# A hybrid diffusion step on one core: low-rank inputs with ScalarE a tile ahead, and two merge branches made inside the recurrent output's stage

## What is computed

```
z = modulate(x, shift1, scale1) @ w_in
z_rw, z_cv, z_q, z_k, z_v, z_gate = split(z)
# recurrent branch, per direction d:
z_rw = z + mu_prev * (z_prev - z) + mu_next * (z_next - z)      # token shift
decay = exp(-0.607 * sigmoid(rw_w0[d] + tanh(zw) @ rw_w2[d]))
a     = sigmoid(rw_a0[d] + za @ rw_a2[d])
k_d   = k * (1 + (a - 1) * rw_k_a)
bonus = sum(r * k * rw_r_k) * v ;  kk = normalize(k * rw_k_k)
y_rw  = (group_norm(scan(...)) + bonus) * (sigmoid(zg) @ rw_g2)
# merge
g_a, g_b, g_c = split(sigmoid(z_gate))
merged = g_a*(y_rw @ w_out_rwkv) + g_b*(y_cv @ w_out_conv) + g_c*(y_at @ w_out_attn)
x = x + gate1 * (merged @ w_o)
x = x + gate2 * peer_ffn(modulate(x, shift2, scale2))
```

## Time and profile before

| what | us |
|---|---|
| median of the runs | 6358.67 |
| lowest and highest of 3 runs | 6358.47, 6360.23 |
| the profiled execution's own time | 6360.67 |
| its span, first to last instruction | 6358.8 |
| PE busy in the span | 5276.5 |
| DVE busy | 3789.7 |

### The profile page before, as it was taken

One profiled execution on the slowest core, in us unless ns is written; L12 is line 12 of the kernel. 1 busy time (PEld: TensorE's weight loads), 2 busy tenths in 40 slices (PEclk: granted clock), 3 DMA queues, 4 the chain that ended last, 5 costly groups with the idle time before them and its releaser, 6 DMA issues. The chain is left out here.

```text
span 6358.8 us, 68926 instructions
## 1 busy us (share of the span) xinstructions
PE 5276.5 (83%) x25836; PEld 2786.5 (44%) x25836; DVE 3789.7 (60%) x8443; ACT 1299.4 (20%) x3116; POOL 1496.5 (24%) x1408
## 2 busy tenths in 40 slices
PE   7998799896987877778789987998968877777777
PEld 3555488453333333333345554884533333333333
DVE  3544566435677777777534445664256777777775
ACT  1022211112222222222111222111022222222221
POOL 0100000002444444444300000000024444444443
PEclk9999899998999899989999998998989999999998
DMA  3112501335999999999831135113359999999998
GB/s 126 67 58 110 215 31 47 147 116 225 420 420 419 406 419 413 417 410 414 356 110 65 58 128 197 40 39 148 115 238 420 420 419 411 418 409 417 410 419 354
DMA packets 325587, 1664.17 MB, mean 262 GB/s; under 512 B 36072, under 2 KB 69096, under 8 KB 159616
## 3 DMA queue, kind: packets, MB, share of 16 engines
q0 software_dynamic: 193504, 1370.70, 52.3%
q1 hardware_dynamic: 131744, 289.00, 12.5%
HBM read 1585.80 MB, written 73.79 MB: 261 GB/s over the span
## 5 line engine op out<-in xcount | busy, mean ns | idle before, releaser
L2008 PE MATMUL psum<-peer_rows,peer_diagonal 128*128 128x512 f32 x5120 | 2512.5, 643 | 703.5 <-ACT peer_diagonal L2052 703.5
L1960 POOL DMA_INDIRECT peer_rows<-in_peer_rows,peer_index x1280 | 1428.8, 1116 | 3361.3 <-PE psum L2008 1737.7
L2151 DVE CUSTOM_DVE_ANT_0 peer_rows<-peer_rows,h_rows 128x1024 f32<-128x1024 f32 x1280 | 1546.7, 1224 | 839.9 <-DMA peer_rows<-in_peer_rows,peer_index 836.8
L2008 PEld LDWEIGHTS psum<-peer_rows,peer_diagonal 128*128 128x128 f32 x5120 | 1020.3, 205 | 2116.2 <-issue 1211.5
L2052 ACT ACTIVATE peer_diagonal<-ident_sb,peer_weight 128x128 f32<-128x128 f32 x1280 | 409.3, 390 | 705.0 <-DVE peer_weight L2123 698.2
L2046 ACT ACTIVATE peer_active<-peer_dots 128x4 f32<-128x4 f32 x320 | 65.7, 205 | 1643.1 <-DVE peer_dots L2151 1643.1
L468 PE MATMUL psum<-in_weights,h_sb 128*128 128x512 f32 (+1 forms) x800 | 309.9, 549 | 0.0
L968 PE MATMUL psum<-h_sb,rw_in_gate_weights 128*128 128x512 f32 (+1 forms) x768 | 232.1, 469 | 84.3 <-ACT y_rw L1003 57.9
L521 DVE SCALAR_TENSOR_TENSOR conv_acc<-conv_in,conv_taps,conv_acc 128x655 f32<-128x655 f32 x240 | 216.4, 901 | 8.5
L468 PEld LDWEIGHTS psum<-in_weights,h_sb 128*128 128x128 f32 x800 | 152.0, 190 | 158.1 <-issue 154.0
L968 PEld LDWEIGHTS psum<-h_sb,rw_in_gate_weights 128*128 128x128 f32 x768 | 133.5, 220 | 187.1 <-issue 94.1
(11 more groups left out here) (345 smaller groups left out, 6167.5 us busy)
## 6 DMA issues: line engine op xcount, KB each, us to landing
rw_out_mod_weights<-in_w_mod SPq DMA_DIRECT2D x16, 2048.0 KB
in_weights<-in_w_in SPq DMA_DIRECT2D x12, 2048.0 KB, 8.5
peer_rows<-in_peer_rows,peer_index POOLq DMA_INDIRECT x1280
modulation_weights<-in_w_mod SPq DMA_DIRECT2D x8, 2048.0 KB
scratch_rw_scratch<-rw_in_direction SPq DMA_DIRECT2D x20, 768.0 KB, 3.6
wkv_own<-scratch_rw_scratch SPq DMA_DIRECT2D x20, 768.0 KB, 6.8
merge_gates<-scratch_gate_scratch SPq DMA_DIRECT2D x16, 960.0 KB
rw_in_gate_weights<-in_w_gate POOLq DMA_DIRECT2D x24, 512.0 KB, 6.0
```

Source lines behind the costliest of these rows:

```text
L1960: nc.gpsimd.indirect_dma_start(rows[spot][:, :], None, t.dram["peer_rows"], bass.IndirectOffsetOnAxis(ap=index[j % 4][:, k:k + 1], axis=0) ...
L2008: last = nc.tensor.matmul(t.bank[2 * (i % 2) + c], diagonal[k % DIAGONALS][:, :], rows[spot][:, D + c * 512:D + (c + 1) * 512], start=(j = ...
L2151: v.tensor_tensor_reduce(rows[spot][:, 0:D], rows[spot][:, 0:D], h[:, :], 1.0, 0.0, ALU.mult, ALU.add, dots[b][:, k:k + 1]).then_inc(s["do ...
```

## The change

It has two parts, and a moved buffer.

1. **Inputs.** The token shift of the low-rank rows moves into the attention stage: DVE does it in six pieces between the units (three instructions a piece, into the new tile `lora_mixed`). In the inputs' stage PE adds the rows `W0` and `A0` itself, by a matmul with one row of ones after each low-rank matmul, so that the two adds of DVE go and ACT reads PSUM. ACT's order becomes: sigmoids, scales, copy of the g2 product, empty(2i), square, root, the low-rank tile of the next token tile, empty(2i+1). DVE makes the bonus's products while ACT squares. PE's first gate comes alone, and products(i) is followed by gate(2i+1) and gate(2i+2).
2. **Output and merge.** The convolution and attention branches of the merge (conv, attn) are made in the output's stage, one block of columns before each chunk of the modulation; DVE gates them into `t.merged`. The modulation's weights get two buffers for four. The merge's stage keeps the recurrent branch alone: 4 matmuls for each i and g, with the weights and gates loaded in two parts.

```diff
@@ attention_stage
+        LORA_UNITS = [(HEADS + 1 + 3 * n, j, g) for n, (j, g) in enumerate((j, g) for j in range(3) for g in range(2))]
+            sp.dma_start(mu_lora[:, :, :], t.dram["mu_lora"][layer, :, :, :]).then_inc(s["mu_loaded"], 16)
+            def shift_lora(j, g):
+                (lo, m), at = GROUPS[g], LORA_PAD[g]
+                out = t.lora_mixed[:, j, lo:lo + m]
+                shifted.step(nc.vector.tensor_scalar(out, t.lora[:, j, at:at + m], mu_lora_own[:, j:j + 1], None, ALU.mult))
+                for k, begin in enumerate((at - 1, at + 1)):
+                    shifted.step(nc.vector.scalar_tensor_tensor(out=out, in0=t.lora[:, j, begin:begin + m], scalar=mu_lora[:, k, j:j + 1], in1=out,
+                                                                op0=ALU.mult, op1=ALU.add))
...
@@ rwkv_inputs_stage
-                if i:
-                    pe.wait_ge(s["vector"], VECTOR.after("a1", i - 1))
-                for d in range(2):
-                    b = d * HD
-                    nc.tensor.matmul(t.bank[d][:, :], lora_tile[b:b + HD, 0, :], w2[b:b + HD, :], start=True, stop=True)
-                for d in range(2):
-                    b = d * HD
-                    nc.tensor.matmul(t.bank[2 + d][:, :], lora_tile[b:b + HD, 1, :], a2[b:b + HD, :], start=True, stop=True)
+                for first, row, j, low_rank in ((2, A0, 1, a2), (0, W0, 0, w2)):
+                    for d in range(2):
+                        b = d * HD
+                        nc.tensor.matmul(t.bank[first + d][:, :], lora_tile[b:b + HD, j, :], low_rank[b:b + HD, :], start=True, stop=False)
+                        nc.tensor.matmul(t.bank[first + d][:, :], t.ones[0:1, :], rows[0:1, row + d, :], start=False, stop=True)
...
             for i in range(TILES):
+                act.wait_ge(s["products"], i + 1)
                 if i:
+                    act.wait_ge(s["vector"], VECTOR.after("key1", i - 1))
+                for d in range(2):
+                    nc.scalar.activation(a[:, d, :], t.bank[2 + d][:, :], ACT.Sigmoid).then_inc(s["scalar"], 1)
...
-                    done.step(v.tensor_tensor(per[d][:, 0, :], t.bank[d][:, :], rows[:, W0 + d, :], ALU.add))
-                    done.step(v.tensor_tensor(a[:, d, :], t.bank[2 + d][:, :], rows[:, A0 + d, :], ALU.add))
@@ rwkv_output_stage
-        mod_weights = [sbuf(f"mod_weights{b}", KD, 512) for b in range(4)]
+        gates, out_weights, product = both("gates", 2, NTOK), both("out_weights", 2, 4, P), sbuf("product", LAT)
+        mod_weights = [sbuf(f"mod_weights{b}", KD, 512) for b in range(2)]
...
+            def load_branch(n):
+                if n >= 2:
+                    sp.wait_ge(s["branch"], 3 * (n - 1))
+                sp.dma_start(out_weights[n % 2][:, :, :, :], t.dram["w_out"][layer, n, :, 1:3, :, :]).then_inc(weights_loaded[n % 2], 16)
+                if n >= 2:
+                    sp.wait_ge(s["gated"], 6 * (n - 1))
+                sp.dma_start(gates[n % 2][:, :, :], t.dram["gate_scratch"][3 * n + 1:3 * n + 3, :, :].rearrange("r p n -> p r n")).then_inc(gates_loaded[n % 2], 16)
...
+            for n in range(KD):
+                load_branch(n)
+                if n == 0:
+                    sp.dma_start(rows[:, :, :], t.dram["rw_rows"][layer, 7:9, :].partition_broadcast(P)).then_inc(s["rows_loaded"], 16)
+                if n < TILES:
+                    load_tile(n)
+                modulation_load(sp, t, s, layer, chunks, mod_weights, mod_bias, n)
...
+            for n in range(KD):
+                branch(n)
+                modulation_product(nc, pe, t, s, chunks, mod_weights, mod_bias, n)
+                if n:
+                    modulation_spread(nc, pe, t, s, chunks, mod_rows, pick, n - 1)
+                if 1 <= n <= TILES:
+                    turn(n - 1)
...
+            for n in range(KD):
+                act.wait_ge(gates_loaded[n % 2], 16 * (n // 2 + 1))
+                nc.scalar.activation(gates[n % 2][:, :, :], gates[n % 2][:, :, :], ACT.Sigmoid).then_inc(s["sigmoid"], 1)
+                if n < TILES:
...
+                modulation_copy(nc, act, t, s, mod_rows, n)
+                if n:
+                    modulation_store(nc, act, t, s, chunks, n - 1)
@@ merge_stage
-        units = [(i, g, r) for i in range(KD) for g in range(2) for r in range(3)]
+        units = [(i, g) for i in range(KD) for g in range(2)]
+        parts = ((0, FIRST), (FIRST, KD))
```

More of the change, by code:

```diff
@@ L1697, in turn, with gate @@
                 dve.wait_ge(s["turned"], i + 1)
-                v.tensor_copy(t.y_rw[:, :, i * P:(i + 1) * P], t.bank[i % 2].rearrange("p (j n) -> p j n", j=4)).then_inc(s["y_copied"], 1)
+                v.tensor_copy(t.y_rw[:, :, i * P:(i + 1) * P], turn_bank.rearrange("p (j n) -> p j n", j=4)).then_inc(s["y_copied"], 1)
+            def gate(n):
+                dve.wait_ge(s["sigmoid"], n + 1)
+                for r, (g, source) in enumerate((g, source) for g, source in ((1, branch_banks), (0, (context_bank[:, 0:P], context_bank[:, P:2 * P])))):
+                    lo, m = GROUPS[g]
+                    out = t.merged[:, n, lo:lo + m]
+                    dve.wait_ge(s["branch"], 3 * n + (1 if g else 3))
+                    v.tensor_tensor(out, gates[n % 2][:, 0, lo:lo + m], source[0][:, 0:m], ALU.mult).then_inc(s["gated"], 1)
+                    if g:
+                        dve.wait_ge(s["branch"], 3 * n + 2)
+                    dve.wait_ge(s["gated"], 6 * n + 3 * r + 1)
+                    v.tensor_tensor(product[:, 0:m], gates[n % 2][:, 1, lo:lo + m], source[1][:, 0:m], ALU.mult).then_inc(s["gated"], 1)
+                    dve.wait_ge(s["gated"], 6 * n + 3 * r + 2)
+                    v.tensor_tensor(out, out, product[:, 0:m], ALU.add).then_inc(s["gated"], 1)
+                dve.wait_ge(s["gated"], 6 * n + 6)
             for i in range(TILES):
+                gate(i)
                 done = Steps(dve, s["vector"], i * len(VECTOR.names))
@@ L1721, in _ @@
                     turn(i - 1)
+            gate(TILES)
             turn(TILES - 1)
+            for n in range(TILES + 1, KD):
+                gate(n)
             dve.wait_ge(s["y_copied"], TILES)
-RWKV_OUTPUT = ("rows_loaded", "loaded0", "loaded1", "turned", "vector", "scalar", "picked", "y_copied", *MOD_SIGNALS)
+RWKV_OUTPUT = ("weights_loaded0", "weights_loaded1", "gates_loaded0", "gates_loaded1", "branch", "gated", "sigmoid", "rows_loaded", "loaded0", "loaded1", "turned", "vector", "scalar", "picked", "y_copied", *MOD_SIGNALS)
 def merge_stage(nc, t, s, before, layer):
-    UNITS = 6
     BANKS = 8
+    FIRST = 2
     with ExitStack() as mem:
@@ L1767, in _ @@
         def _(pe):
-            for n, (i, g, r) in enumerate(units):
+            for n, (i, g) in enumerate(units):
                 lo, m = GROUPS[g]
-                if n % UNITS == 0:
-                    pe.wait_ge(weights_loaded[i % 2], 16 * (i // 2 + 1))
+                if g == 0 and i in (0, FIRST):
+                    pe.wait_ge(weights_loaded[i // FIRST], 16)
                 if n >= BANKS:
@@ L1774, in _ @@
                 for k in range(4):
-                    last = nc.tensor.matmul(t.bank[n % BANKS][:, 0:m], out_weights[i % 2][:, r, k, :], branches[r][:, k, lo:lo + m],
-                                            start=(k == 0), stop=(k == 3))
+                    last = nc.tensor.matmul(t.bank[n % BANKS][:, 0:m], out_weights[:, i, k, :], t.y_rw[:, k, lo:lo + m], start=(k == 0), stop=(k == 3))
                 last.then_inc(s["product"], 1)
             pe.wait_ge(s["gated"], len(units))
-            pe.wait_ge(s["added"], KD * 4)
+            pe.wait_ge(s["added"], len(units))
             pe.wait_ge(s["last_loaded"], 32)
```

206 lines of the change are left out of this document (97 added, 109 removed).

## The result

The changed kernel takes 6390.47 us (median of 5 runs, 6386.47 to 6396.73) beside 6359.51 for the kernel before (5 runs on the same chip): a ratio of 1.0044, 95% interval 1.0033 to 1.0056. It is 31 us slower, where 40 us less had been forecast. Its profiled execution took 6396.73 us, with a span of 6395.0.

A forecast was written before the change was run, and what follows sets the result against it. PE bounds attention, output and merge; in the inputs' stage engines take turns, and PE would set the pace after the change. Saving 2 x (12.0 + 7.7) = 39.4 from 6360.67 gives 6321.3 profiled, median 6319, range 6294 to 6341.

The forecast's parts named there:

- rival 3: Inputs' stage: PE still waits 29.0 us for copies out of bank 7; +9.3 us a layer, median 6377; chance 0.04.
- the 3 us either way: Output and merge stages: the margin given to their net -7.7 us a layer, for moved turns and chunk 0's landing.
- the one-row term: Inputs' stage, low-rank products: nine matmuls of alternating shapes run in series at 0.96 us each, 8.6 us a tile.
- the forecast 148.7: Inputs' stage, PE's first to last gate: 12 x 8.65 + 5 x 8.6 + 1.9 = 148.7 us, against 160.7 before.
- Rival 2: Inputs' stage: clock falls once a tile in the low-rank products, making them 10.7 us; -9.2 a layer, median 6340; chance 0.08.
- Rival 1: Inputs' stage: one-row matmuls overlap, products 6.1 us a tile; -32.2 us a layer in all, median 6294.3; chance 0.26.

The follow-up runs named there:

- the spreads apart: Changed kernel with identity bias matmuls first, plus the output stage's modulation spread moved ahead of the next chunk's product: 6296.99 us, 0.9891 of the kernel before.

## Why the prediction was wrong

**What held.** PE's waits for `y_rw` went, 29.0 to 0 (rival 3 did not come). PE became the stage's bound. Output and merge: the merge fell by 70.4 us (forecast 69.3), the output's stage grew by 63.0 (61.6), net -7.4 against -7.7 in the first layer. Chunk 0's product began 16.1 us after the stage's first transfer (forecast 15.9), since its weights landed about when forecast (16.1 for 15.7); PE's first matmul came after 3.6 us and not 5.1, and PE then waited 1.9 us for these weights. Attention stayed within 0.1 us, and DVE's shift there cost 8.4 us of busy time (estimate 9) that nobody waited for. The second layer's output stage was 4.7 us longer than the first's, more than the 3 us either way. Rows of PE in it that read 7.03, 3.60 and 3.60 at the full clock:

```profile
4403.82 8.72 PE L156 MATMUL psum<-rw_out_mod_weights,silu_sb 128*2 128x512 f32 x16 [2.24 <-DMA rw_out_mod_bias<-in_b_mod]
...
4433.19 4.62 PE L1685 MATMUL psum<-y_conv,rw_out_out_weights 128*128 128x512 f32 x8
...
4454.10 6.11 PE L1685 MATMUL psum<-y_conv,rw_out_out_weights 128*128 128x512 f32 x8
```

The first is a slow start behind a wait, the others follow the few-row spreads: 5.2 us together. In the first layer the same three rows read 7.03, 3.60 and 4.80, 1.2 us together. With the spreads apart no such row is low; what makes the clock fall behind one spread of a stage and not behind another is open.

**The step that failed** is the one-row term, "in series: 9 x 0.96 = 8.6 us a tile". It was too small in three ways, worked out here for the first layer:

- Matmuls of two alternating shapes start 1.05 us apart at the full clock, not 0.96: 9.2 - 8.6 = 0.6 a tile, 3.0 us a layer. The row used for 0.96 has a different neighbour on one side only.
- The clock fell in every tile: 14.0 - 9.2 = 4.8, 24.0 us a layer.
- The gates behind ran on at the low level for a while: 18.56 - 17.47 = 1.1 in the first tile, 0.8 to 1.9 in the others, 6.4 us a layer.

Together 33.4 of the 34.2 us by which PE's run from first to last gate (587.9 to 770.8, 182.9 us) exceeds the forecast 148.7.

**Rival 2 had the right mechanism at the wrong price.** It was given 0.08 and 2.1 us a tile; the runs show 6.1, the fall and the slower gates (4.8 + 1.3). The 2.1 came from a row (9.12 for 7.03) of a start behind a wait, where the clock was about to rise; the other row (8.72) was a fall in the middle of work, but a short one. Here the fall lasted through all that was left of the group and some of what follows. The bound for "the clock falls" should have been the whole group at half speed: 2 x 9.2 = 18.4 us a tile, a range whose upper end is slower than before. The argument against it, that seven of eight chunks with a one-row matmul kept the clock, compared one such matmul behind eight of 128 rows with four among nine.

**Rival 1**, the overlap, did not occur with one-row matmuls, but it does with 64-row ones: then the gain exceeds what rival 1 promised (ratio 0.9873, where 6294 of 6359 us is 0.990).

The sum closes, from the forecast 6321.3 us for the profiled execution: + 33.6 and + 33.8 (inputs' stages, +21.6 and +21.8 for -12.0) + 0.3 + 4.8 (output and merge of the two layers) = 6393.8, measured 6396.7. The stages that the change does not touch hold the other 3 us.

**A rule of the pages.** The Trainium skill, "TensorE: Matmul & The Clock Gate", section "What's actually happening", has the clock set by how busy the engine has recently been, and the section "HAM oscillation — how this bites in real kernels" looks for its fall in idle gaps. The trace disagrees with the second: 0.50 granted with PE busy 10.90 of 10.90 us. It neither confirms nor refutes the first, since no run here shows what the chip takes for busy. "TensorEngine Tiling (Array Packing)", "Key Properties", has a change of tiling mode drain the engine; the 1.05 us from start to start of alternating shapes (64 and 128 rows), against 0.88 for four 128-row ones in a row, agrees.

## What to carry to other kernels

A bias row folded into a matmul as one row of ones looks free in operations, and it isn't: several such matmuls close together can halve the clock of the work around them. Widen the stationary operand with zero rows to the shape of its neighbours, against a bias spread over as many partitions, so that the matmuls overlap and the clock stays. Or leave the addition on an engine with room: with the copies' order adapted to it, that was the fastest version here. And when a clock fall is possible, let the upper bound be the whole group at half speed, not the difference of one row.

## What the hardware showed that I had not expected

- The granted clock falls to 0.50 under continuous work when several matmuls close together span few rows: ten of ten tiles with single-row ones alternating, eight of ten with them grouped, none of ten where the same bias was added by instructions that span 64 or 128 rows. Zeros in 63 of the stationary operand's 64 rows did not bring it down.
- One single-row and two two-row matmuls in a row did the same in the output's stage: a fall in each of 16 stages, in none of six where 128-row matmuls stand between the two kinds.
- A product pair and a bias pair of 64 rows, each matmul onto the bank that its half has just written, start 0.86 to 0.96 us apart; in the kernel before, two pairs onto different banks start 0.96 apart (728.46 to 729.42). So accumulating onto the bank just written did not hold up the pairs.
